# One comparison for both one-hots of an expert gate table, read by TensorE with a 32 byte step, and the table spread over eight weight tiles instead of twelve

## The chip, the cores and the metric

The kernel runs on one core of one Trainium2 chip. The metric is the device time of a whole run in microseconds (us). TensorE (PE, with its weight loads as PEld), VectorE (DVE), ScalarE (ACT), GpSimd (POOL) and the engine that issues weight transfers (SP) run side by side and wait for one another through semaphores.

## The reference, cut to what matters

The program is two transformer blocks on 512 tokens of width 1024. The change lies in the expert layer of the first block:

```python
scores = jnp.einsum('bshpc,hpnc->bshpn', q, sub_keys)        # 8 heads, 2 halves, 128 keys each
top_s, top_i = lax.top_k(scores, PEER_TOPK)                  # 16 best keys of each half
cand_i = top_i[..., 0, :, None] * 128 + top_i[..., 1, None, :]
best_s, best_pos = lax.top_k(cand_s, PEER_TOPK)              # 16 best pairs of each head
gate = jax.nn.softmax(best_s, axis=-1)
u = jnp.take(expert_u, ib, axis=0)                           # 128 experts for a token, of 16384
act = gelu(jnp.einsum('td,tkd->tk', xb, u))
y = jnp.einsum('tk,tkd->td', gb * act, jnp.take(expert_v, ib, axis=0))
```

## The kernel before

The first 128 tokens gather their expert rows. The other 384 (`ND`) run through all 16384 experts: `act` is computed densely as weight tiles times the tokens, and multiplied by a table of gates that is zero where a token did not choose an expert. This table is made one token at a time. A token has 128 choices (the partitions), each with a first key, a second key and a gate. With `hot1` the one-hot of the first key and `hot2` that of the second, the 128x128 matmul of `hot2` (the stationary operand) and `hot1` times the gate (the moving operand) gives the token's gates for all 16384 experts.

The stage `experts_u` streams 64 tiles of the first half of the work. One tile (`early_tile`, `part_u`, L1163 to L1183) is 24 fp32r matmuls of 128x384. Weights come from SP into a ring of four slots; ACT rounds a slot to its high part (`split_slot`, L795), POOL or DVE subtracts for the low part, and both parts are multiplied. ACT takes each finished tile through Gelu (`early_gelu`, L1932), splits the slot four tiles on and stores the result. The stage `experts` then streams further tiles in steps of six slots: two more tiles of activations (`late_tile`) and four slots of expert rows (`share`, L1230), which need the gates back from DRAM.

Meanwhile DVE picks the keys (`route_block`, four blocks of 128 tokens). PE transposes each block's keys and gates (`indices`, L1194), and DVE keeps them (`keep`, L2578) as `idx1`, `idx2` and `gate_t`. Tiles 0 to 51 run beside that. Tiles 52 to 63 (`G_TURN` = 13 turns of 4) carry the table, eight batches of four tokens in each: after every chunk of three matmuls, PE does four tokens (`g_batch`, L1209). A token's fp32 matmul shows as two MATMUL records. Batches go in groups of eight tokens, 48 groups in all, in double buffers:

- DVE (`hot_group`): first keys against `key_of`, all bf16, stored keys by tokens (L2703, 1024 elements); second keys against the key numbers in f32, stored tokens by keys (L2706, 1024 elements); then first one-hot times gate for four of the eight tokens (L2709, 512 elements), reading bf16 with a step of eight elements.
- ACT (`scale_hot`, L1960): the same product for the other four tokens, one instruction of 128 elements each, with the same step. Then it copies two batches of four tokens from PSUM to the staging buffer (L1976), and every fourth group it stores 2048 KB of gates (L1980).
- DVE also makes one low part of a weight slot per tile (`low_early_slot`, L2718), since POOL is occupied with gathers there.

DVE makes the constant `key_of` (L2722) just ahead of its first group. After the last group ACT waits for all stored gates and all stored activations, fetches the first gates and activations back (L1986, L1990), and only then takes the first `late_tile` through Gelu (L1999). PE's third late tile waits for that. DVE multiplies activations by gates (L2767) and makes low parts (L2772); the first `share` waits for these. Order on each engine is the program's order; every wait is a semaphore written by hand.

Of the kernel before, what the change touches and what calls it, by code (L numbers as in the profile page):

```python
# [36 lines left out]
P = 128  # L37
D = 1024
DC = D // P
# [76 lines left out]
GROUP = 2 * BATCH  # L116
QUAD = 4 * STEP
GBUFS = 6
SCALED = 4
DOT_STEPS = NSEL // 8  # L120
LOG_SEQ = 9
PADS = 5
# [45 lines left out]
def build(nc, c_d, ada_d, stream, consts_d, vecs_d, tables_d, x_d, keys_d, u_rows, v_rows, chunks_d, act_d, gates_d, out_d):  # L168
    with ExitStack() as ctx:
# [37 lines left out]
        def view(at, *dims, dt=F32, rows=P, of=None):  # L207
            n = int(np.prod(dims))
            of = of if of is not None else arena_r if dt == F32R else arena
            assert at + n <= of.shape[1], (at, dims, of.shape)  # L210
            a = of[0:rows, at:at + n]
            if dt == U32:
                a = a.bitcast(dt)
            if len(dims) == 2:
                a = a.rearrange("p (a b) -> p a b", b=dims[1])
            if len(dims) == 3:
                a = a.rearrange("p (a b c) -> p a b c", b=dims[1], c=dims[2])
            if len(dims) == 4:
                a = a.rearrange("p (a b c d) -> p a b c d", b=dims[1], c=dims[2], d=dims[3])
            return a  # L220
# [51 lines left out]
        yg = view(1056, D)  # L272
        routed = [view(1056 + 384 * k, 3, NSEL) for k in range(2)]
        pos_abf = view(1824, 2, NSEL)
        idx2 = view(2112, ND)
        gate_t = view(2496, ND)
        idx1 = place("idx1", [P, ND], BF16, at=at_arena + 2880)
        eidx = view(3264, NSEL, dt=U32)
        gate_g = view(3392, NSEL)
        act_g = view(3520, NSEL)  # L280
# [12 lines left out]
        keys = view(23656, QH, NKEYS)  # L293

        g_stage = [view(4448 + 4096 * k, NKEYS, STEP) for k in range(2)]
        hot2 = view(12640, 2, GROUP, NKEYS)
        hot1g = view(14688, 2, GROUP, NKEYS)
        hot1 = [place(f"hot1_{k}", [P, NKEYS, GROUP], BF16, at=at_arena + 16736 + 512 * k) for k in range(2)]
        key_of = place("key_of", [P, NKEYS, GROUP], BF16, at=at_arena + 17760)
        g_rows = [view(19552 + D * k, D) for k in range(GBUFS)]  # L300

        early = view(4448, 2, 2, ND)
# [208 lines left out]
        routed_ready = sem("routed_ready")  # L511
        eidx_ready = sem("eidx_ready")
        hot1_made = sem("hot1_made")
        hot_scaled = sem("hot_scaled")
        rows_in = [sem(f"rows_in{k}") for k in range(GBUFS)]
        rows_used = sem("rows_used")
        dots_taken = sem("dots_taken")
# [371 lines left out]
        def _(pe):  # L889
# [307 lines left out]
            for b in range(1, TB):  # L1197
                span(pe, INDEX_TURNS[b - 1], INDEX_TURNS[b], early_turn)
                indices(b)
            pe.wait_ge(h_row_ready, 1)  # L1200

            def g_batch(n, group, k):

                pe.wait_ge(hot_ready, group + (k // 2 + 1))
                pe.wait_ge(hot_scaled, group + (k // 2 + 1))
                wait(pe, g_kept, n + (k - 3))
                for t in range(BATCH):
                    at_t = BATCH * (k % 2) + t
                    last = pe.matmul(ps[:, k % 4, t * P:(t + 1) * P], hot2[:, k // 2 % 2, at_t, :],  # L1209
                                     hot1g[:, k // 2 % 2, at_t, :], start=True, stop=True)  # L1210
                last.then_inc(g_made, 1)

            def g_steps(i):
                for s in range(RING):
                    early_tile(i + G_TURN, s, lambda k: g_batch(i * 32 + DC * s, i * 16 + 4 * s, k))
            turns(pe, 3, g_steps)

            def late_tile(i, j, turn, s):
                wait(pe, gelu_done, i * 2 + (TILES + j - 1))
# [485 lines left out]
        def _(act):  # L1705
# [245 lines left out]
                act.activation(best[b % 2], best[b % 2], ACT.Exp).then_inc(gate_exp, 1)  # L1951


            def scale_hot(g):

                act.wait_ge(hot1_made, g + 1)
                wait(act, g_made, 2 * (g - 1))
                for t in range(SCALED):
                    k = GROUP * g + t
                    last = act.activation(hot1g[:, g % 2, t, :], hot1[g % 2][:, :, t], ACT.Identity,  # L1960
                                          scale=gate_t[:, k:k + 1])
                last.then_inc(hot_scaled, 1)

            groups = ND // GROUP
            scale_hot(0)
            for g in range(groups):
                step, n = g // 4, 2 * g
                if g % 4 == 0:
                    wait(act, g_saved[step % 2], 16 * (step // 2))
                if g + 1 < groups:  # L1970
                    scale_hot(g + 1)
                for k in (n, n + 1):
                    if k % DC == DC - 1:
                        early_gelu(G_TURN + step // RING, step % RING)
                    act.wait_ge(g_made, k + 1)
                    act.activation(g_stage[step % 2][:, :, BATCH * (k % DC):BATCH * (k % DC + 1)],  # L1976
                                   ps[:, k % 4, :].rearrange("p (t i) -> p i t", i=NKEYS), ACT.Copy).then_inc(g_kept, 1)
                if g % 4 == 3:
                    act.wait_ge(g_kept, n + 2)
                    act.dma_start(gates_d[:, step, :], g_stage[step % 2].rearrange("p i t -> p (i t)"))\  # L1980
                        .then_inc(g_saved[step % 2], 16)


            def fetch_gates(q):
# [20 lines left out]

            for k in range(2):
                act.wait_ge(g_saved[k], 16 * (STEPS // 2))
                act.wait_ge(act_saved[k], 16 * (TILES // 2))
            fetch_gates(0)
            fetch_acts(0)  # L2010
            for j in range(2):
                late_gelu(0, j, used(t0, j))
            for j in range(2):
                high_gated(j, late_hi[:, 0, j, :], late[:, j, :])
            for i in range(last_step):
                k0 = 2 + 6 * i
                p = i % 2
                wait(act, act_split, i * 4)
                fetch_acts(i + 1)
                if i == DOT_STEPS:  # L2020
                    act.wait_ge(rows_used, NSEL)
                    act.activation(act_g, act_g, ACT.Gelu).then_inc(dots_taken, 1)
                if p == 0 and i // 2 + 1 < TILES // 4:
                    fetch_gates(i // 2 + 1)
                split_expert(k0 + 2)
                split_expert(k0 + 3)
                for j in range(2):
                    high_gated(i * 4 + (2 + j), early_hi[:, j, :], early[:, p, j, :])
                for j in range(2):
                    late_gelu(i + 1, j, used(t0, k0 + j))  # L2030
                    split_expert(k0 + 4 + j)
                for j in range(2):
                    high_gated(i * 4 + (4 + j), late_hi[:, 1 - p, j, :], late[:, j, :])
                split_expert(k0 + 6)
                split_expert(k0 + 7)
# [316 lines left out]
        def _(dve):  # L2352
# [221 lines left out]
            def keep(b):  # L2574

                dve.wait_ge(routed_t, b)
                for k, dst in enumerate((idx1, idx2, gate_t)):
                    dve.tensor_copy(dst[:, (b - 1) * P:b * P], ps[:, 6, k * P:(k + 1) * P]).then_inc(routed_kept, 1)  # L2578

            steps = [0]  # L2580
# [23 lines left out]
            def route_block(b):  # L2604
# [79 lines left out]
                if b == 0:  # L2684
                    after()
                    dve.scalar_tensor_tensor(eidx, to[:, 0, :], float(NKEYS), to[:, 1, :], ALU.mult, ALU.add)\
                        .then_inc(eidx_ready, 1)

            for b in range(TB):
                route_block(b)  # L2690
                if b == TB - 1:
                    finish_gates(b)
                if b >= 2:
                    keep(b - 1)
            keep(TB - 1)

            def hot_group(g):

                t = slice(GROUP * g, GROUP * (g + 1))
                wide = [P, GROUP, NKEYS]  # L2700
                iota = cst("iota").unsqueeze(1).broadcast_to(wide)
                wait(dve, hot_scaled, g - 1)
                dve.tensor_tensor(hot1[g % 2][:, :, :], idx1[:, t].unsqueeze(1).broadcast_to([P, NKEYS, GROUP]), key_of[:, :, :],  # L2703
                                  ALU.is_equal).then_inc(hot1_made, 1)
                wait(dve, g_made, 2 * (g - 1))
                dve.tensor_tensor(hot2[:, g % 2], idx2[:, t].unsqueeze(2).broadcast_to(wide), iota, ALU.is_equal)  # L2706
                dve.wait_ge(hot1_made, g + 1)
                rest = slice(GROUP * g + SCALED, GROUP * (g + 1))
                dve.tensor_tensor(hot1g[:, g % 2, SCALED:, :], hot1[g % 2][:, :, SCALED:].rearrange("p j t -> p t j"),  # L2709
                                  gate_t[:, rest].unsqueeze(2).broadcast_to([P, GROUP - SCALED, NKEYS]), ALU.mult)\  # L2710
                    .then_inc(hot_ready, 1)

            def low_early_slot(k):

# [4 lines left out]
                    .then_inc(lo_ready, 1)  # L2719

            dve.wait_ge(routed_kept, 3 * (TB - 1))
            dve.tensor_copy(key_of[:, :, :], cst("iota").unsqueeze(2).broadcast_to([P, NKEYS, GROUP])).then_inc(routed_kept, 1)  # L2722
            dve.wait_ge(routed_kept, 3 * (TB - 1) + 1)
            for g in range(ND // GROUP):
                hot_group(g)
                if g % 4 == 1 and g > 4:
                    low_early_slot(g // 4 - 1)
            low_early_slot(ND // GROUP // 4 - 1)


            rows_done = [0]
# [585 lines left out]
```

## Time and profile before

| what | value |
|---|---|
| median of 3 runs | 3136.06 us (3135.14 to 3137.20) |
| span of the profiled execution, first to last instruction | 3134.2 us |
| PE busy / DVE / ACT / POOL | 95% / 65% / 40% / 37% |
| mean granted TensorE clock | 0.979 of full speed |

The page gives the span of the profiled execution and no separate time around it; the span is 1.9 us under the median of the runs. Busy shares are means over stages with quite different limits, so the stage that the change touches (from 738 us to 927 us of the span) is read by itself.

### The profile page before, as it was taken

The page shows a single profiled execution, that of the slowest core. Times are in us where ns is not written, and L with a number is a line of the kernel's source. Part 1 is how long each engine was busy: PE and PEld are TensorE (multiplying, and loading weights), DVE is VectorE, ACT ScalarE, POOL GpSimd, SP SyncE. Part 2 cuts the span into 40 slices and gives each one's busy share as a digit, 9 for nine tenths or more (in the row PEclk, how much of TensorE's full clock was granted, in tenths as well). Part 3 has the DMA queues.
Part 4 walks back from the last instruction along what each step waited for, and adds up shares of the span by engine and source line. Part 5 has one row for each costly group of instructions (what it writes and reads, how often), then busy time and mean ns, then how long its engine had stood idle before and what let it go on. Part 6 is the DMA issues. An engine that isn't in the chain of part 4 may idle for free.

```text
span 3134.2 us, 47541 instructions
## 1 busy us (share of the span) xinstructions
PE 2990.2 (95%) x17673; PEld 2612.4 (83%) x17673; DVE 2025.2 (65%) x3238; ACT 1261.6 (40%) x2075; POOL 1157.7 (37%) x564
## 2 busy tenths in 40 slices
PE   6999999998999999999999999899999998999998
PEld 3766679998988888888887788699999975799986
DVE  4767515999977778788886255466651375466622
ACT  3347333446963333333333334432222446432221
POOL 2420333664014444455553222044444430244442
PEclk9998999999999999999999999799999999999999
DMA  6710223555679999999996211023223420122231
GB/s 247 280 60 1 62 93 96 166 175 191 227 248 350 346 328 341 337 351 350 346 347 229 75 55 41 14 88 94 87 88 101 117 81 1 41 89 93 94 101 67
DMA packets 179876, 509.22 MB, mean 162 GB/s; under 512 B 14881, under 2 KB 72353, under 8 KB 175393
## 3 DMA queue, kind: packets, MB, share of 16 engines
q1 hardware_dynamic: 72288, 262.57, 25.4%
q0 software_dynamic: 37440, 136.40, 11.9%
q10 hardware_dynamic: 70016, 108.54, 10.3%
q8 instruction: 79, 1.29, 0.2%
q14 instruction: 53, 0.43, 0.0%
HBM read 467.60 MB, written 39.85 MB: 162 GB/s over the span
## 4 chain that ended last, share of the span: by engine, by line
PE 87%; ACT 5%; DVE 4%; issue 2%; DMA 1%; ACTq 0%; DVEq 0%
PE ps L1279 23%; PE ps L1230 17%; PE ps L1167 16%; PE ps L1533 8%; PE ps L901 8%; ACT arena L1960 2%; PE ps L1351 2%; PE ps L952 1%; ACT arena L1976 1%; PE ps L1680 1%; PE ps L1299 1%; PE ps L1457 1%; PE ps L1414 1%; PE ps L654 1%; PE ps L1421 1%
## 5 line engine op out<-in xcount | busy, mean ns | idle before, releaser
L2314 POOL TENSOR_TENSOR w_lo<-ring,w_hi 128x1024 fp32r<-128x1024 f32 x300 | 755.0, 2520 | 1387.9 <-ACT w_hi L795 1387.8
L795 ACT ACTIVATE w_hi<-ring 128x1024 fp32r<-128x1024 f32 x500 | 525.4, 1055 | 771.9 <-PE ps L1230 277.4
L1230 PE MATMUL ps<-w_hi,arena_r 128*128 128x512 f32 x1536 | 426.8, 397 | 4.5 <-DVE arena_r L2772 4.5
L1167 PE MATMUL ps<-h_hi,w_hi 128*128 128x384 f32 x1024 | 355.5, 347 | 5.0 <-issue 5.0
L1230 PEld LDWEIGHTS ps<-w_hi,arena_r 128*128 128x128 f32 x1536 | 289.0, 189 | 72.2 <-DVE arena_r L2772 5.0
L1167 PE MATMUL ps<-h_lo,w_hi 128*128 128x384 f32 x1024 | 348.9, 341 | 0.0
L1279 PE MATMUL ps<-h_hi,w_hi 128*128 128x264 f32 (+2 forms) x1536 | 347.5, 298 | 0.6 <-DVE arena L2869 0.5
L1167 PE MATMUL ps<-h_hi,w_lo 128*128 128x384 f32 x1024 | 346.4, 338 | 0.0
L1279 PE MATMUL ps<-h_lo,w_hi 128*128 128x264 f32 (+2 forms) x1536 | 346.2, 297 | 0.0
L1279 PE MATMUL ps<-h_hi,w_lo 128*128 128x264 f32 (+2 forms) x1536 | 345.6, 297 | 0.0
L2327 POOL DMA_INDIRECT arena<-u_rows,arena x128 | 193.4, 1511 | 375.8 <-DVE arena L2748 354.5
L2761 DVE TENSOR_TENSOR w_lo<-ring,w_hi 128x1024 fp32r<-128x1024 f32 x188 | 228.4, 1221 | 134.9 <-ACT w_hi L795 133.6
L2327 POOL DMA_INDIRECT arena<-v_rows,arena x128 | 206.6, 1614 | 174.8 <-DVE arena L2754 143.9
L1279 PEld LDWEIGHTS ps<-h_hi,w_hi 128*128 128x128 f32 x1536 | 246.6, 188 | 10.5 <-DVE arena L2869 0.9
L1279 PEld LDWEIGHTS ps<-h_hi,w_lo 128*128 128x128 f32 x1536 | 243.9, 189 | 7.5
L1279 PEld LDWEIGHTS ps<-h_lo,w_hi 128*128 128x128 f32 x1536 | 244.0, 188 | 6.6
L1230 PE MATMUL ps<-w_lo,arena_r 128*128 128x512 f32 x768 | 241.9, 397 | 0.0
L1533 PE MATMUL ps<-arena_r,w_hi 128*128 128x264 f32 (+1 forms) x1056 | 224.5, 321 | 0.0
L1167 PEld LDWEIGHTS ps<-h_hi,w_hi 128*128 128x128 f32 x1024 | 193.7, 189 | 6.6 <-issue 5.3
L1167 PEld LDWEIGHTS ps<-h_lo,w_hi 128*128 128x128 f32 x1024 | 193.9, 189 | 1.4
L1167 PEld LDWEIGHTS ps<-h_hi,w_lo 128*128 128x128 f32 x1024 | 194.3, 190 | 0.0
L1533 PEld LDWEIGHTS ps<-arena_r,w_hi 128*128 128x128 f32 x1056 | 163.3, 188 | 15.9
(343 smaller groups left out, 5444.0 us busy)
## 6 DMA issues: line engine op xcount, KB each, us to landing
ring<-weight_stream SPq DMA_DIRECT2D x500, 512.0 KB, 3.7
gates<-arena ACTq DMA_DIRECT2D x12, 2048.0 KB, 7.3
arena<-gates ACTq DMA_DIRECT2D x32, 768.0 KB, 14.3
arena<-w_modulation ACTq DMA_DIRECT2D x17, 1024.0 KB, 5.3
early_acts<-arena ACTq DMA_DIRECT2D x64, 192.0 KB, 2.7
arena<-early_acts ACTq DMA_DIRECT2D x32, 384.0 KB, 7.7
arena<-w_modulation ACTq DMA_DIRECT2D x2, 2560.0 KB, 15.0
x<-x_t ACTq DMA_DIRECT2D x1, 2112.0 KB, 19.5
```

Of the source, the lines that this page charges most:

```text
L654: last = pe.matmul(dst if n.T == SEQ else dst[:, b, :], lhsT, src[:, lo:hi], start=j == 0, stop=j == len(group) - 1)
L795: act.activation(w_hi[:, s, :], ring[:, s, :], ACT.Copy).then_inc(hi_ready, 1)
L901: last = pe.matmul(ps[:, bank, :], w, v, start=c == 0 and p == 0, stop=c == DC - 1 and p == 2)
L1167: last = pe.matmul(ps[:, bank, 0:ND], w, v, start=c == 0 and p == 0, stop=c == DC - 1 and p == 2)
L1230: last = pe.matmul(ps[:, Y_BANKS[b][half], :], a[u], w[v][:, half * BANK:(half + 1) * BANK], start=first and p == 0, stop=final and p == 2)
L1279: last = pe.matmul(ps[:, 2 * pair + b, 0:hi - lo], w, v[:, lo:hi], start=c == 0 and p == 0, stop=c == DC - 1 and p == 2)
L1351: last = pe.matmul(ps[:, v_bank(half, b), :], v, w, start=c == 0 and p == 0, stop=c == DC - 1 and p == 2)
L1533: last = pe.matmul(ps[:, 2 * (t % 2) + b, 0:hi - lo], w, v[:, lo:hi], start=c == 0 and p == 0, stop=c == FC - 1 and p == 2)
L1960: last = act.activation(hot1g[:, g % 2, t, :], hot1[g % 2][:, :, t], ACT.Identity, scale=gate_t[:, k:k + 1])
L2314: pool.tensor_tensor(w_lo[:, s, :], ring[:, s, :], w_hi[:, s, :], ALU.subtract)\
L2327: pool.indirect_dma_start(out=g_rows[n % GBUFS], out_offset=None, in_=table, in_offset=bass.IndirectOffsetOnAxis(ap=eidx[:, s:s + 1], axis ...
L2761: dve.tensor_tensor(w_lo[:, s, :], ring[:, s, :], w_hi[:, s, :], ALU.subtract).then_inc(lo_ready, 1)
```

## The change

- `idx1` and `idx2` are both kept as bf16 in one tile `idx12`. One comparison makes both one-hots of eight tokens (`compare_keys`, 2048 elements, bf16 in and out, keys by tokens).
- DVE multiplies all eight first one-hots by their gates (`scale_keys`, 1024 elements, read and written keys by tokens), and waits for the comparison of that group. ACT no longer scales; it widens the second one-hots to f32 with one copy of 1024 elements (`widen_hot`).
- `hot1g` and `hot2` are stored keys by tokens, so PE reads one token of either with a step of eight f32 elements (32 bytes), both as stationary and as moving operand.
- The table starts at tile 54 and takes eight tiles with twelve batches each. Tiles 52, 53, 62 and 63 carry none. ACT takes tiles 52 and 53 through Gelu before its first widening.
- `key_of` is made before `route_block(0)`. DVE's eight low parts go to every sixth group and four follow after the loop.
- After the table ACT fetches the first gates without waiting for all stored activations; for the first activations it waits for two stores, and for the others after the first late Gelu.

```diff
-        idx2 = view(2112, ND)
-        idx1 = place("idx1", [P, ND], BF16, at=at_arena + 2880)
+        idx12 = place("idx12", [P, 2, ND], BF16, at=at_arena + 2880)
+        key_of = place("key_of", [P, NKEYS, GROUP], BF16, at=at_arena + 3776)
-        hot2 = view(12640, 2, GROUP, NKEYS)
-        hot1g = view(14688, 2, GROUP, NKEYS)
+        hot2 = view(12640, 2, NKEYS, GROUP)
+        hot1g = view(14688, 2, NKEYS, GROUP)
+        hot = [place(f"hot{k}", [P, 2, NKEYS, GROUP], BF16, at=at_arena + 16736 + 1024 * k) for k in range(2)]
...
+            for s in range(2):
+                early_tile(G_TURN, s)
...
-                    last = pe.matmul(ps[:, k % 4, t * P:(t + 1) * P], hot2[:, k // 2 % 2, at_t, :],
-                                     hot1g[:, k // 2 % 2, at_t, :], start=True, stop=True)
+                    last = pe.matmul(ps[:, k % 4, t * P:(t + 1) * P], hot2[:, k // 2 % 2, :, at_t],
+                                     hot1g[:, k // 2 % 2, :, at_t], start=True, stop=True)
...
+                def batches(c):
+                    per = G_BATCHES // G_TILES
+                    for k in range(per * c // DC, per * (c + 1) // DC):
+                        g_batch(per * j + k)
...
-            def scale_hot(g):
-                act.wait_ge(hot1_made, g + 1)
-                wait(act, g_made, 2 * (g - 1))
-                for t in range(SCALED):
-                    k = GROUP * g + t
-                    last = act.activation(hot1g[:, g % 2, t, :], hot1[g % 2][:, :, t], ACT.Identity,
-                                          scale=gate_t[:, k:k + 1])
+            def widen_hot(g):
+                act.wait_ge(hot1_made, g + 2)
+                wait(act, g_made, 2 * (g - 1))
+                act.activation(hot2[:, g % 2], hot[g % 2][:, 1], ACT.Copy).then_inc(hot_widened, 1)
...
-            scale_hot(0)
+            for t in range(G_TURN * RING, G_FIRST):
+                early_gelu(t // RING, t % RING)
+            widen_hot(0)
...
-                act.wait_ge(act_saved[k], 16 * (TILES // 2))
             fetch_gates(0)
+            for k in range(2):
+                act.wait_ge(act_saved[k], 16)
             fetch_acts(0)
...
+            def compare_keys(g):
+                t = slice(GROUP * g, GROUP * (g + 1))
+                both = [P, 2, NKEYS, GROUP]
+                wait(dve, hot_widened, g - 1)
+                dve.tensor_tensor(hot[g % 2][:, :, :, :], idx12[:, :, t].unsqueeze(2).broadcast_to(both),
+                                  key_of[:, :, :].unsqueeze(1).broadcast_to(both), ALU.is_equal).then_inc(hot1_made, 1)
+            def scale_keys(g):
+                t = slice(GROUP * g, GROUP * (g + 1))
+                dve.wait_ge(hot1_made, g + 2)
+                wait(dve, g_made, 2 * (g - 1))
+                dve.tensor_tensor(hot1g[:, g % 2], hot[g % 2][:, 0],
+                                  gate_t[:, t].unsqueeze(1).broadcast_to([P, NKEYS, GROUP]), ALU.mult).then_inc(hot_ready, 1)
...
+            compare_keys(0)
+            lows = 3 * RING
             for g in range(ND // GROUP):
-                hot_group(g)
-                if g % 4 == 1 and g > 4:
-                    low_early_slot(g // 4 - 1)
+                scale_keys(g)
+                if g + 1 < ND // GROUP:
+                    compare_keys(g + 1)
+                if g % 6 == 2:
+                    low_early_slot(g // 6)
```

## Rows read from the trace of the kernel before

**Rows 1.** The page, busy time of each engine.

```profile
PE 2990.2 (95%) x17673; PEld 2612.4 (83%) x17673; DVE 2025.2 (65%) x3238; ACT 1261.6 (40%) x2075; POOL 1157.7 (37%) x564
```

**Rows 2.** Windows of the table: PE, PEld, DVE, ACT, POOL busy, clock, DMA share, GB/s.

```profile
752.00:754.00 2.00, 2.00 (x10) 2.00 (x9) 1.67 (x3) 1.24 (x3) 0.00 (x0) 0.50 0.00 0
826.00:839.00 13.00, 12.12 (x94) 11.80 (x93) 12.82 (x15) 12.51 (x29) 0.00 (x0) 1.00 0.59 219
```

**Rows 3.** The chain that ended last, 735 to 930 us: start, length, what.

```profile
831.02 0.96 ACT arena L1976 x2
831.99 1.67 ACT arena L1960 x4
...
902.04 8.46 PE ps L1167 x48
910.50 5.01 issue
915.50 11.34 PE ps L1167 x48
```

**Rows 4.** The same chain over the whole span, in the expert stage.

```profile
943.64 8.44 PE ps L1167 x48
```

**Rows 5.** Groups of instructions by form, 517 to 960 us.

```profile
L1209 PE MATMUL ps<-arena 128*128 128x128 f32 x768 | 103.6, 278 | 16.3 <-ACT arena L1960 7.1 <-DVE arena L2709 5.4 <-issue 3.8
...
L1960 ACT ACTIVATE arena<-hot,arena 128x128 f32<-128x128 bf16 x192 | 85.2, 522 | 13.3 <-DVE hot L2703 8.0 <-ACT arena L1976 5.3
...
L2706 DVE TENSOR_TENSOR arena<-arena,const 128x1024 f32<-128x1024 f32 x48 | 58.7, 1224 | 3.8 <-PE ps L1209 2.1
...
L2709 DVE TENSOR_TENSOR arena<-hot,arena 128x512 f32<-128x512 bf16 x48 | 51.7, 1078 | 0.0
L2703 DVE TENSOR_TENSOR hot<-idx,key_of 128x1024 bf16<-128x1024 bf16 x48 | 33.0, 687 | 0.0
...
L1951 ACT ACTIVATE arena<-arena 128x128 f32<-128x128 f32 x4 | 1.2, 310 | 0.0
```

**Rows 6.** Timeline of DVE in one table tile: start, length, engine, line.

```profile
829.18 1.21 DVE L2718 TENSOR_TENSOR w_lo<-ring,w_hi 128x1024 fp32r<-128x1024 f32 x1
830.31 0.68 DVE L2703 TENSOR_TENSOR hot<-idx,key_of 128x1024 bf16<-128x1024 bf16 x1
830.92 1.21 DVE L2706 TENSOR_TENSOR arena<-arena,const 128x1024 f32<-128x1024 f32 x1
```

**Rows 7.** Timeline of PE in one table tile.

```profile
831.26 1.15 PE L1209 MATMUL ps<-arena 128*128 128x128 f32 x8 [0.88 <-ACT arena L1960]
...
834.20 1.05 PE L1209 MATMUL ps<-arena 128*128 128x128 f32 x8
...
835.62 1.05 PE L1209 MATMUL ps<-arena 128*128 128x128 f32 x8
```

**Rows 8.** Timeline of ACT in one table tile.

```profile
827.22 1.06 ACT L795 ACTIVATE w_hi<-ring 128x1024 fp32r<-128x1024 f32 x1
...
828.16 0.60 ACT L1976 ACTIVATE arena<-ps 128x512 f32<-128x512 f32 x1
```

**Rows 9.** Timeline at the start of the table.

```profile
743.19 0.87 PE L1194 MATMUL ps<-const,arena 128*128 128x128 f32 x3 [5.02 <-DVE arena L2578]
...
744.82 2.69 DVE L2722 CAST key_of<-const 128x1024 bf16<-128x1024 f32 x1
...
750.39 2.08 PE L1209 MATMUL ps<-arena 128*128 128x128 f32 x8 [5.37 <-DVE arena L2709]
```

**Rows 10.** Timeline of ACT after the table.

```profile
903.14 0.33 ACTq L1980 DMA_DIRECT2D gates<-arena  x1
910.79 1.53 ACTq L1986 DMA_DIRECT2D arena<-gates  x2
```

**Rows 11.** Timeline of DVE after the table.

```profile
918.90 1.03 DVE L2767 TENSOR_TENSOR arena<-arena 128x384 f32<-128x384 f32 x2 [15.02 <-DMA arena<-gates]
...
925.32 1.02 DVE L2772 TENSOR_TENSOR arena_r<-arena,arena_r 128x384 fp32r<-128x384 f32 x2
```

More of the change, by code:

```diff
@@ L118 @@
 GBUFS = 6
-SCALED = 4
+G_TILES = 8
+G_FIRST = 54
 DOT_STEPS = NSEL // 8
@@ L295, in build @@
         g_stage = [view(4448 + 4096 * k, NKEYS, STEP) for k in range(2)]
-        hot2 = view(12640, 2, GROUP, NKEYS)
-        hot1g = view(14688, 2, GROUP, NKEYS)
-        hot1 = [place(f"hot1_{k}", [P, NKEYS, GROUP], BF16, at=at_arena + 16736 + 512 * k) for k in range(2)]
-        key_of = place("key_of", [P, NKEYS, GROUP], BF16, at=at_arena + 17760)
+        hot2 = view(12640, 2, NKEYS, GROUP)
+        hot1g = view(14688, 2, NKEYS, GROUP)
+        hot = [place(f"hot{k}", [P, 2, NKEYS, GROUP], BF16, at=at_arena + 16736 + 1024 * k) for k in range(2)]
         g_rows = [view(19552 + D * k, D) for k in range(GBUFS)]
@@ L513, in build @@
         hot1_made = sem("hot1_made")
-        hot_scaled = sem("hot_scaled")
+        hot_widened = sem("hot_widened")
         rows_in = [sem(f"rows_in{k}") for k in range(GBUFS)]
@@ L1199, in _, with g_batch, g_between @@
                 indices(b)
+            for s in range(2):
+                early_tile(G_TURN, s)
             pe.wait_ge(h_row_ready, 1)
[L1202 to L1206, printed above, removed]
+            def g_batch(k):
+                pe.wait_ge(hot_ready, k // 2 + 1)
+                pe.wait_ge(hot_widened, k // 2 + 1)
+                wait(pe, g_kept, k - 3)
                 for t in range(BATCH):
                     at_t = BATCH * (k % 2) + t
-                    last = pe.matmul(ps[:, k % 4, t * P:(t + 1) * P], hot2[:, k // 2 % 2, at_t, :],
-                                     hot1g[:, k // 2 % 2, at_t, :], start=True, stop=True)
+                    last = pe.matmul(ps[:, k % 4, t * P:(t + 1) * P], hot2[:, k // 2 % 2, :, at_t],
+                                     hot1g[:, k // 2 % 2, :, at_t], start=True, stop=True)
                 last.then_inc(g_made, 1)
[L1213 to L1216, printed above, removed]
+            def g_between(j):
+                def batches(c):
+                    per = G_BATCHES // G_TILES
+                    for k in range(per * c // DC, per * (c + 1) // DC):
+                        g_batch(per * j + k)
+                return batches
+            for j in range(G_TILES):
+                early_tile((G_FIRST + j) // RING, (G_FIRST + j) % RING, g_between(j))
+            for t in range(G_FIRST + G_TILES, TILES):
+                early_tile(t // RING, t % RING)
             def late_tile(i, j, turn, s):
@@ L1951, in _ @@
                 act.activation(best[b % 2], best[b % 2], ACT.Exp).then_inc(gate_exp, 1)
-            def scale_hot(g):
-                act.wait_ge(hot1_made, g + 1)
+            def widen_hot(g):
+                act.wait_ge(hot1_made, g + 2)
                 wait(act, g_made, 2 * (g - 1))
-                for t in range(SCALED):
-                    k = GROUP * g + t
-                    last = act.activation(hot1g[:, g % 2, t, :], hot1[g % 2][:, :, t], ACT.Identity,
-                                          scale=gate_t[:, k:k + 1])
-                last.then_inc(hot_scaled, 1)
+                act.activation(hot2[:, g % 2], hot[g % 2][:, 1], ACT.Copy).then_inc(hot_widened, 1)
             groups = ND // GROUP
-            scale_hot(0)
+            for t in range(G_TURN * RING, G_FIRST):
+                early_gelu(t // RING, t % RING)
+            widen_hot(0)
             for g in range(groups):
@@ L1970, in _ @@
                 if g + 1 < groups:
-                    scale_hot(g + 1)
+                    widen_hot(g + 1)
                 for k in (n, n + 1):
-                    if k % DC == DC - 1:
-                        early_gelu(G_TURN + step // RING, step % RING)
+                    per = G_BATCHES // G_TILES
+                    if k % per == per - 2:
+                        early_gelu((G_FIRST + k // per) // RING, (G_FIRST + k // per) % RING)
                     act.wait_ge(g_made, k + 1)
@@ L1981, in _ @@
                         .then_inc(g_saved[step % 2], 16)
+            for t in range(G_FIRST + G_TILES, TILES):
+                early_gelu(t // RING, t % RING)
             def fetch_gates(q):
@@ L2014, in _ @@
                 high_gated(j, late_hi[:, 0, j, :], late[:, j, :])
+            for k in range(2):
+                act.wait_ge(act_saved[k], 16 * (TILES // 2))
             for i in range(last_step):
@@ L2576, in keep @@
                 dve.wait_ge(routed_t, b)
-                for k, dst in enumerate((idx1, idx2, gate_t)):
+                for k, dst in enumerate((idx12[:, 0], idx12[:, 1], gate_t)):
                     dve.tensor_copy(dst[:, (b - 1) * P:b * P], ps[:, 6, k * P:(k + 1) * P]).then_inc(routed_kept, 1)
@@ L2687, in route_block @@
                         .then_inc(eidx_ready, 1)
+            dve.tensor_copy(key_of[:, :, :], cst("iota").unsqueeze(2).broadcast_to([P, NKEYS, GROUP])).then_inc(hot1_made, 1)
             for b in range(TB):
@@ L2695, in _ @@
             keep(TB - 1)
-            def hot_group(g):
+            def compare_keys(g):
                 t = slice(GROUP * g, GROUP * (g + 1))
[L2700 to L2704, printed above, removed]
-                wait(dve, g_made, 2 * (g - 1))
[L2706 to L2711, printed above, removed]
+                both = [P, 2, NKEYS, GROUP]
[5 more added lines that the diff above has]
+                dve.wait_ge(hot1_made, g + 2)
+                wait(dve, g_made, 2 * (g - 1))
+                dve.tensor_tensor(hot1g[:, g % 2], hot[g % 2][:, 0],
+                                  gate_t[:, t].unsqueeze(1).broadcast_to([P, NKEYS, GROUP]), ALU.mult).then_inc(hot_ready, 1)
             def low_early_slot(k):
@@ L2721, in _ @@
             dve.wait_ge(routed_kept, 3 * (TB - 1))
-            dve.tensor_copy(key_of[:, :, :], cst("iota").unsqueeze(2).broadcast_to([P, NKEYS, GROUP])).then_inc(routed_kept, 1)
-            dve.wait_ge(routed_kept, 3 * (TB - 1) + 1)
+            dve.wait_ge(hot1_made, 1)
+            compare_keys(0)
+            lows = 3 * RING
             for g in range(ND // GROUP):
-                hot_group(g)
-                if g % 4 == 1 and g > 4:
-                    low_early_slot(g // 4 - 1)
-            low_early_slot(ND // GROUP // 4 - 1)
+                scale_keys(g)
[3 more added lines that the diff above has]
+                    low_early_slot(g // 6)
+            for k in range(ND // GROUP // 6, lows):
+                low_early_slot(k)
             rows_done = [0]
```

## The prediction

> **What bounds the kernel now.** I read the page first. It says PE, 95% busy [rows 1], but that is a mean over all stages, so I read the stage of the change by itself, first in windows and in the chain, then on each engine's timeline.
>
> In a table tile PE, DVE and ACT are all nearly full: 12.12, 12.82 and 12.51 of 13 us [rows 2]. Which of them ends last is in the chain: ACT, with 1.67 us for four scalings and 0.96 us for two copies in every group [rows 3]. PE's own pace is a batch start to start when nothing is late: 835.62 - 834.20 = 1.42 us [rows 7]. Once or more in a tile PE waits, as 0.88 us on ACT's scaling [rows 7]. From the first table matmul at 750.39 [rows 9] to the last at 902.04 [rows 3] are 151.7 us; 96 batches of 1.42 us are 136.3. So 15.4 us are lost inside the table.
>
> Two more losses lie around it. At the start PE waits 5.02 us for routing (that stays), does the transposes at 743.19, and then waits 5.37 us more for the first group, while DVE makes `key_of` in 2.69 us [rows 9]; its clock is still 0.50 at 752 to 754 us, the lower of its two levels (1.2 and 2.4 GHz), and 1.00 later [rows 2]. At the end the last gates leave at 903.14 and the fetch goes out at 910.79 [rows 10], with ACT's Gelu queued behind it, so PE idles 5.01 us; its next two tiles take 11.34 us where two such tiles in the expert stage take 8.44 [rows 3, 4]. These 2.9 us are the price of the slow clock after a pause. In the expert stage the chain is PE work alone [rows 4], so what is saved here should come through to the end whole.
>
> **Part by part.** *PE.* A chunk of three weight matmuls is 3 x 8.46/48 = 0.529 us [rows 3]. A token costs (1.42 - 0.529)/4 = 0.223 us, and each of its two records 0.111 us. The count of both stays, so PE's work from tile 52 to 63 stays 136.3 us, if reading with a 32 byte step costs nothing. Not one PE operand before has such a step, so I bound it. DVE reads bf16 with a 16 byte step in L2709. Its fixed part comes from L2706 and L2703: 1224 - 687 = 537 ns is half of 1024 elements' streaming in f32, so 1.05 ns each and 150 ns fixed. L2709 then takes (1078 - 150)/512 = 1.81 ns for an element [rows 5]. ACT takes 522 ns for 128 such elements, against 310 for 128 adjacent ones: 1.66 ns more on top of about 0.9, so 2.55 [rows 5, 8]. PE streams adjacent fp32r at 0.176/384 = 0.46 ns [rows 3] and this fp32 table at 0.111/128 = 0.87 ns. The two ends: by ratio, DVE's slowing of 1.7 on PE's best rate is 0.79 ns, below 0.87, so nothing is added (there is no reason for a gain); by absolute time, ACT's 2.55 ns makes a record 0.326 us, and 768 records [rows 5] cost 768 x 0.215 = 165 us. I take nothing, because the table's fp32 stream asks for elements only about half as often as PE is seen to read them; but this is the weak step.
>
> "Need at least two hits on a cacheline to absorb SRAM access latency", says the Trainium skill (Advanced Engine Details and Errata, SBUF Cachelines), with lines of 16 bytes. By that rule a 32 byte step pays; the DVE and ACT rows agree for their 16 byte step, and no row here shows it for TensorE. It gives no size; with DVE's row for the price, the sum would be about 3204 us instead of 3113.5.
>
> *DVE.* Away go a bf16 comparison (0.61 us start to start), an f32 comparison (1.13, as any plain 1024 here) [rows 6] and the stepped product (1078 ns) [rows 5]. In come a comparison of 2048 bf16 elements, 150 + 2 x 537 = 1224 ns, if it keeps the double rate of L2703, and a product of 1024 adjacent elements at 1.13. The product now waits for the comparison just ahead of it, so that one counts in full, with an allowance of 0.04 us to wake. A group is 1.13 + 1.26 = 2.39 us; six are 14.3, and the low part adds 1.13 but hides one wait: 15.3 us a tile. PE's new tile is 8 x 0.529 + 48 x 0.223 = 14.9. DVE is late by 0.4 a tile, 3.2 in eight; double buffers let it be 2.49 - 1.22 = 1.3 us ahead at most. I take 2 us.
>
> *ACT.* A group is one copy of 1024 (0.94 us, the pitch of L795 [rows 8]) and two of 512 (0.96 [rows 3]): six are 11.4, with Gelu (0.35 by its 384 elements), split (0.94) and the gate store 13.6 of 14.9 us. After the Gelu of a tile the widening of the group after next comes 5.0 us after PE ends the tile, and PE wants it after about 4.6; that is within the allowance for DVE. Nothing.
>
> *Start.* `key_of` moves to where DVE waits for the first scores, which costs nothing; without that pause it would be 2.69 us in front of the routing. Tiles 52 and 53 fill PE's 5.37 us. PE starts them cold: 2.9 us lost, as after the other pause. But ACT's first widening is now queued behind tile 53's Gelu and split, 0.35 + 0.94 + 1.06 = 2.4 us after that tile, and PE has one chunk of 0.53 to cover it: 1.9 us lost.
>
> So from the end of the transposes at 743.7 (743.19 and about 0.5): 136.3 + 2.9 + 1.9 + 2 = 143.1 us, where 902.04 - 743.7 = 158.3 were spent. Saved: 15.2.
>
> *End.* The store of the last gates takes 903.14 to 910.79, 7.65 us, and now lies beside tiles 62 and 63 (8.46 us). ACT then has tile 63's Gelu and split, fetches at about 10 us after tile 61, and the first late Gelu comes at about 14, while PE wants it after four tiles, 16.9. The fetch to the second early low part took 926.34 - 910.79 = 15.6 us [rows 10, 11]; so the first `share` is ready at 25.5 and PE has six tiles, 25.4. DVE's 15.02 us of waiting for gates [rows 11] becomes harmless. From the last table matmul to the first share PE needed 8.46 + 5.01 + 11.34 = 24.8; now 16.9 and 0.5 for collisions with the store. Saved: 7.4. Stores of gates (12) and activations stay the same in number, in 119 us instead of 152; SP and POOL get their low parts two tiles ahead as before.
>
> Sum: 3136.1 - 15.2 - 7.4 = 3113.5 us, on the median; the span it is read from is 1.9 us less.
>
> **Rivals.**
> 1. *TensorE pays for the step* (ends slower). For it: two engines of two that read a 16 byte step pay. Against it: PE's fp32 stream is at half its seen rate. If a record doubles, 768 x 0.111 = +85 and DVE's 2 us vanish: 3197. By DVE's 1.81 ns a record is 0.232: +93, 3204. By ACT's ratio of 2.8 on 0.46 ns it is 0.165: +42, 3153. By ACT's absolute time 3277. It decides from 22.6/768 = 29 ns a record, 1.1 ns an element. The cacheline rule of the Trainium skill (page and section above) speaks for this rival.
> 2. *The merged comparison loses the double rate.* Then 150 + 2048 x 1.05 = 2300 ns; a group 3.47, 48 of them and eight low parts 174.6 against PE's 119.2: +55 for the 2: 3167. Against it: the same operand pattern runs at it in L2703 [rows 5], with one dimension less.
> 3. *The saving is smaller.* The engines, again within 10% of one another, go on waiting in turn and lose the 15.4 us again: 3127. Or the fetch still ends last: 7.4 back, 3121.
>
> **How the numbers follow.** The forecast 0.53, its own range 3104 to 3122 (DVE never late, no end collision, and less cold time below; ACT late by 0.5 a tile and 2 us at the end above). Rival 1 0.36, rival 2 0.04, rival 3 0.05, others 0.02. The range must take in doubling and DVE's price: 3104 to 3205 leaves out under 0.04 below and 0.11 above. A measurement here tells about 0.2%, 6 us. Faster: 0.53 and most of rival 3, 0.57. Slower: rivals 1 and 2 without their mildest cases, 0.39. Same: 0.04.
>
> **What the profile of the changed kernel would show.** The matmul records of the table line start 0.11 us apart, or 0.2 and more: this alone decides the sign. The merged comparison takes 1.22 us and not 2.3; the product 1.22; ACT's widening 1.06. PE has no idle time from the transposes to tile 54's first chunk, then some 1.9 us for ACT. Between table and first share it shows no pause and no fall of the clock. The forecast is wrong if PE's records stretch, or if the widening rather than DVE's product ends last in each group.

## The result, and the profile after

The changed kernel takes 3215.11 us (median of 4 runs, 3211.62 to 3219.31) where the kernel before takes 3135.6 us: 1.0256 times as long, 95% interval 1.0243 to 1.0269. It is slower by 2.6%, outside the range that was forecast. The forecast had the sign wrong.

The groups of instructions after, 517 to 1040 us (count, then busy us, mean ns, idle before); they stand against those of the products and comparisons before [rows 5]:

```profile
L1211 PE MATMUL ps<-arena 128*128 128x128 f32 x768 | 196.7, 422 | 2.0 <-ACT arena L1968 2.0
...
L1211 PEld LDWEIGHTS ps<-arena 128*128 128x128 f32 x768 | 189.0, 336 | 2.3 <-issue 2.3
...
L2717 DVE TENSOR_TENSOR hot<-idx,key_of 128x2048 bf16<-128x2048 bf16 x48 | 60.6, 1262 | 4.7 <-ACT arena L1968 4.7
L2725 DVE TENSOR_TENSOR arena<-hot,arena 128x1024 f32<-128x1024 bf16 x48 | 58.8, 1226 | 95.1 <-PE ps L1211 95.0
L1985 ACT ACTIVATE arena<-ps 128x512 f32<-128x512 f32 x96 | 57.3, 597 | 103.2 <-PE ps L1211 103.2
L1968 ACT ACTIVATE arena<-hot 128x1024 f32<-128x1024 bf16 x48 | 50.4, 1052 | 5.3 <-ACT arena L1985 5.3
```

The new work of DVE and ACT costs what was forecast: comparison 1262 ns (1224 forecast), product 1226 ns (about 1220), widening 1052 ns (1060). The double rate of the bf16 comparison is there. But TensorE's table records have grown from 278 to 422 ns each, its weight loads for the table from 193 to 336, and DVE and ACT now wait for PE in place of the reverse: 95.0 and 103.2 us of idle time.

The chain that ended last after, start and length, through the stage:

```profile
742.03 9.93 PE ps L1167 x48
753.32 1.05 ACT arena L1968
754.51 2.25 PE ps L1211 x8
756.76 0.96 PE ps L1167 x3
757.73 3.78 PE ps L1211 x16
...
853.90 3.87 PE ps L1211 x16
...
974.68 8.43 PE ps L1167 x48
...
984.74 10.19 DMA arena<-gates
...
1002.48 7.74 PE ps L1240 x32
```

Sixteen records in 3.87 us are 0.242 us each, against 0.111 before. 768 x 0.131 = 100.6 us. In the chain before, ACT held most of the table [rows 3]; now PE holds it all. A window of the table says the same, with the clock at 1.00 (PE, PEld, DVE, ACT, POOL busy, clock, DMA share, GB/s), and two of the first microseconds of the table show the clock partly or wholly at its lower level:

```profile
754.00:757.00 3.00, 2.49 (x10) 2.52 (x11) 1.23 (x1) 1.51 (x3) 0.00 (x0) 0.74 0.02 5
757.73:758.70 0.97, 0.97 (x5) 0.97 (x5) 0.00 (x0) 0.00 (x0) 0.00 (x0) 0.50 0.00 0
850.00:866.00 16.00, 16.00 (x72) 15.98 (x71) 8.32 (x8) 8.46 (x13) 0.00 (x0) 1.00 0.26 110
```

PE and its loads are full for all 16 us; DVE and ACT are at 8.32 and 8.46.

The early rows say one thing more. For the first 0.97 us of the 16 records that start at 757.73 the clock stood at 0.50, and DVE and ACT did nothing; yet the 16 took 3.78 us, no more than the 3.87 at full clock. The chunk of three weight matmuls just before took 0.96 us where 0.53 is the pace at full clock. So the stepped record does not stretch with the granted clock, as it would if its 0.242 us were so many cycles of TensorE (by estimate that would have added about 0.5 us).

The measure used from here on is the time from the transposes of the last block (L1194) to the first matmul of the first `share`: 743.19 to 926.7 before, 183.5 us; 741.16 to 1002.5 after, 261.3 us. The difference, 77.8 us, is nearly the whole of the difference of the medians, 79.5, so what happens in the stage does pass to the end whole. It stands in this table for every run, beside the start-to-start time of one record in the gate table. A ratio is to runs of the kernel before taken beside it, whose median was 3135.2 to 3137.3 us; the four kernels with one run have none.

| kernel | median us | ratio to before, 95% interval | stage us | record us |
|---|---|---|---|---|
| before | 3135.6 | | 183.5 | 0.111 |
| after, both operands at 32 bytes | 3215.1 | 1.0256 (1.0243 to 1.0269) | 261.3 | 0.242 |
| e2, stationary alone at 32 bytes | 3208.2 (1 run) | | 254.9 | 0.234 |
| e3, moving alone at 32 bytes | 3209.1 (1 run) | | 254.2 | 0.233 |
| e5, both at 16 bytes | 3211.7 (1 run) | | 257.6 | 0.238 |
| e4, both at 8 bytes | 3118.9 (1 run) | | 168.2 | 0.1175 |
| e8, the same again | 3122.2 | 0.9951 (0.9937 to 0.9964) | 169.6 | 0.1175 |
| e1, adjacent for PE, stepped for the writers | 3154.0 | 1.0059 (1.0046 to 1.0073) | 200.7 | 0.111 |
| e6, 8 bytes, twelve tiles | 3128.9 | 0.9973 (0.9962 to 0.9984) | 174.5 | 0.1175 |
| e7, 8 bytes, widening earlier | 3120.8 | 0.9949 (0.9936 to 0.9963) | 165.9 | 0.1175 |
| e9, 8 bytes, tiles 53 to 60 | 3119.8 | 0.9942 (0.9928 to 0.9955) | 165.6 | 0.1175 |

Single runs of one kernel lie up to 9 us from their median, much of it through time outside the stage (the profiled runs of e4 and e8, the same kernel, took 3118.85 and 3131.3 us with 168.2 and 169.6 in the stage), so differences of a few microseconds are read in the stage column.

### The profile page after: what moved, and what is told of

Same layout as the page of the kernel before. It is cut to its first block, busy times and chain, and to the rows that moved or that the text cites. A ratio compares the mean times of both kernels' runs of the same rounds, so it can differ in the third digit from the quotient of the medians.

```text
span 3210.7 us, 47292 instructions
## 1 busy us (share of the span) xinstructions
PE 3085.4 (96%) x17673; PEld 2711.3 (84%) x17673; DVE 2004.4 (62%) x3190; ACT 1235.3 (38%) x1931; POOL 1153.7 (36%) x564
## 4 chain that ended last, share of the span: by engine, by line
PE 91%; DVE 4%; ACT 2%; DMA 1%; issue 1%; ACTq 0%; DVEq 0%
PE ps L1289 23%; PE ps L1240 17%; PE ps L1167 16%; PE ps L1543 8%; PE ps L901 8%; PE ps L1211 6%; PE ps L1361 2%; PE ps L952 1%; PE ps L1690 1%; PE ps L654 1%; PE ps L1309 1%; PE ps L1467 1%; PE ps L1424 1%; PE ps L1431 1%; PE ps L1450 1%
## 5 line engine op out<-in xcount | busy, mean ns | idle before, releaser
L2341 POOL DMA_INDIRECT arena<-v_rows,arena x128 | 205.6, 1606 | 174.5 <-DVE arena L2773 143.6
L1211 PE MATMUL ps<-arena 128*128 128x128 f32 x768 | 196.7, 422 | 2.0 <-ACT arena L1968 2.0
```

The lines of the kernel that those rows point to most:

```text
L2341: pool.indirect_dma_start(out=g_rows[n % GBUFS], out_offset=None, in_=table, in_offset=bass.IndirectOffsetOnAxis(ap=eidx[:, s:s + 1], axis ...
```

## The experiments

All keep the arithmetic of the changed kernel. What is varied in each is first the layout of the two f32 tables: `hot2` and `hot1g` become runs of S tokens. TensorE then reads a token with a step of 4 x S bytes: S = 8 is the changed kernel, S = 1 gives adjacent keys.

```diff
-        hot2 = view(12640, 2, NKEYS, GROUP)
+        hot2 = view(12640, 2, GROUP // S, NKEYS, S)
-  hot2[:, k // 2 % 2, :, at_t]
+  hot2[:, k // 2 % 2, at_t // S, :, at_t % S]
-  act.activation(hot2[:, g % 2], hot[g % 2][:, 1], ACT.Copy)
+  act.activation(hot2[:, g % 2].rearrange("p a j s -> p j a s"),
+                 hot[g % 2][:, 1].rearrange("p j (a s) -> p j a s", s=S), ACT.Copy)
```

and the same for `hot1g` with DVE's product. What PE computes is the same in all of them; only the places of the elements differ.

### e1: adjacent keys for TensorE (S = 1 for both)

> The changed kernel, but ACT's widening and DVE's product write their tables tokens by keys, so that PE reads adjacent elements and the step of 512 bytes is on the writing side. Theory A (TensorE pays for reading with a 32 byte step: its table records start 0.242 us apart after the change against 0.111 before, and 768 x 0.131 = 101 us is the whole miss): records back at 0.111 us, 3215 - 101 = 3114 us, which is the prediction without its weak step. Rival B (the records are long for another reason, such as keys by tokens being in the same SBUF lines that DVE and ACT write at that time): they stay above 0.2 us, near 3215. Rival C (the writers pay for a stepped write as they do for a stepped read, 1.81 ns an element on DVE): DVE's group is 1.26 + 2.0 = 3.3 us, 48 groups 157 + 8 low parts against PE's 119, so about 3155.

Measured: 3154.0 us, and the groups of instructions of this run, 740 to 1000 us:

```profile
L1211 PE MATMUL ps<-arena 128*128 128x128 f32 x768 | 103.7, 282 | 29.0 <-issue 14.5 <-DVE arena L2726 11.4 <-ACT arena L1968 2.9
L1968 ACT ACTIVATE arena<-hot 128x1024 f32<-128x1024 bf16 x48 | 99.4, 2074 | 7.0 <-PE ps L1211 5.3 <-DVE hot L2718 0.9
L2726 DVE TENSOR_TENSOR arena<-hot,arena 128x1024 f32<-128x1024 bf16 x48 | 98.0, 2042 | 4.9 <-PE ps L1211 3.6
```

PE's timeline has the pace of a batch with no wait in it:

```profile
845.72 1.05 PE L1211 MATMUL ps<-arena 128*128 128x128 f32 x8
...
847.14 2.11 PE L1211 MATMUL ps<-arena 128*128 128x128 f32 x16
```

A batch is again 847.14 - 845.72 = 1.42 us start to start, and a record 0.111 us, as before [rows 7]; its mean length is 282 ns (278 before). So the records on TensorE are as theory A has them, and B falls: the read step is what made them long. (Shared lines could not have done it: the writers fill one half of the double buffer while PE reads the other.) But the time is not 3114. The step has moved to the writers, and they pay as rival C said: DVE's product takes 2042 ns in place of 1226, (2042 - 150)/1024 = 1.85 ns an element, and ACT's widening 2074 in place of 1052. In the chain DVE's product and comparison now follow each other, 3.06 us a group. PE waits for DVE's product (11.4 us). The step has a price on whichever side it stands. That the time fell on rival C's 3155 within 1 us is partly chance: its own terms (157 + 9 - 119 us on 3114, less the 2 us that the 3114 already held for DVE's lateness) give about 3159, and a group took 3.06 us and not 3.3.

### e2 and e3: one operand alone (S = 8 and S = 1)

> Only the stationary operand (second keys) is read with the 32 byte step, the moving one is adjacent. Theory A1 (each of the two streams is limited by itself at 1.89 ns an element and loads lie beside the matmuls): records 0.242 us apart, 3215. Rival A2 (the moving stream alone pays): 0.111, 3114. Rival A3 (both pay and the costs add up): half, about 0.177, 3165.

> Only the moving operand (first keys times gates) is read with the 32 byte step. A1: 0.242 us a record, 3215. A2: also 0.242, 3215. A3: 0.177, 3165. If it is 0.111 here, the loads alone pay.

Measured: 3208.2 and 3209.1 us. One row of the chain of e2, then of e3:

```profile
799.70 3.75 PE ps L1211 x16
```

```profile
801.22 3.73 PE ps L1211 x16
```

That is 0.234 and 0.233 us a record: each stepped stream by itself is nearly as slow as both together (0.242). Theory A1 holds; that the moving stream alone pays (A2) and that the costs add up (A3) are both out. Loads lie beside matmuls, and the slower of the two sets the pace, so leaving one of the operands adjacent helps almost nothing. The groups of the two runs, 740 to 1000 us, e2 first, show which is which: the loads are long (334 ns) where the stationary operand is the stepped one and nearly as in e1 (207 against 195) where it is not.

```profile
L1211 PEld LDWEIGHTS ps<-arena 128*128 128x128 f32 x768 | 188.1, 334 | 2.3 <-issue 2.3
L2726 DVE TENSOR_TENSOR arena<-hot,arena 128x1024 f32<-128x1024 bf16 x48 | 95.8, 1995 | 57.2 <-PE ps L1211 56.4
```

```profile
L1211 PEld LDWEIGHTS ps<-arena 128*128 128x128 f32 x768 | 157.2, 207 | 18.7 <-issue 3.2
L1968 ACT ACTIVATE arena<-hot 128x1024 f32<-128x1024 bf16 x48 | 97.2, 2028 | 5.3 <-ACT arena L1986 5.3
```

They also repeat e1's reading: DVE's product, the only one that writes with the long step in e2, takes 1995 ns; ACT's widening in e3 2028.

### e4, e5 and e8: a step of 8 and of 16 bytes

> Both operands are read with a step of 8 bytes (pairs of tokens adjacent), two elements to every 16 bytes. Theory D (what costs is 16 bytes fetched per 1.89 ns, so two elements in 16 bytes take 0.94 ns each against the 0.87 ns that the fp32 stream wants): records 0.121 us, 3114 + 768 x 0.010 = 3122. Theory E (any step loses adjacency and costs the same): 0.242, 3215.

> Both operands are read with a step of 16 bytes (four tokens adjacent), one element to every 16 bytes. Theory D (one 16 byte piece of SBUF per 1.89 ns and stream): the same as the 32 byte step, records 0.242 us apart, 3215 us. Rival F (the cost grows with the length of the step, from 0.1175 at 8 bytes to 0.242 at 32): about 0.16 to 0.18, 3150 to 3165.

> The fourth run's kernel timed in rounds. 3119 us again (3116 to 3122), faster than the kernel before by 0.55%. If the single time was a chance low, it lies nearer to 3136 than 3125.

Measured: 3118.9 us for 8 bytes, 3211.7 for 16, and 3122.2 for 8 bytes again (median of 6 runs), 0.9951 of the kernel before. In e4 the keys of a token lie 8 bytes apart, two in every 16 bytes, with those of another token between them. The chain of e4, then of e5:

```profile
842.78 1.88 PE ps L1211 x16
...
880.85 9.22 DMA gates<-arena
...
890.80 9.04 DMA arena<-gates
...
907.51 17.07 PE ps L1240 x72
```

```profile
773.51 3.80 PE ps L1211 x16
```

It gives 1.88/16 = 0.1175 us a record at 8 bytes (theory D: 0.121), 3.80/16 = 0.238 at 16. Doubling the step from 8 to 16 bytes doubles the time of a record, and doubling it again to 32 adds nothing that matters. So rival F (the cost grows with the length) and theory E (any step costs the same) fall. What the runs fit is one 16 byte piece of SBUF per about 1.9 ns and stream: with two wanted elements in a piece an element takes 0.92 ns, close to the 0.87 ns of the fp32 stream of adjacent keys; with one in a piece 1.86 to 1.89. The size of 16 bytes is what fits, and is not measured by itself: the runs show that a step of 8 bytes is nearly free and one of 16 costs as much as one of 32. "Need at least two hits on a cacheline to absorb SRAM access latency" (the Trainium skill, Advanced Engine Details and Errata, SBUF Cachelines): these runs agree for TensorE, and give the price that the section does not. What inside the memory or the engines sets this pace the runs do not tell, but for the one thing that the pace does not follow TensorE's granted clock (3.78 us for 16 records, part of them at 0.50). The writers of e4, which store two adjacent elements and then hop 1 KB, pay little, DVE 5 ns of 1226 and ACT 126 ns of 1052:

```profile
L2726 DVE TENSOR_TENSOR arena<-hot,arena 128x1024 f32<-128x1024 bf16 x48 | 59.1, 1231 | 7.2 <-PE ps L1211 5.7
L1968 ACT ACTIVATE arena<-hot 128x1024 f32<-128x1024 bf16 x48 | 56.5, 1178 | 5.9 <-ACT arena L1986 3.4 <-PE ps L1211 1.9 <-DVE hot L2718 0.2
```

### e6: the table over twelve tiles again, at 8 bytes

```diff
-G_TILES = 8
-G_FIRST = 54
+G_TILES = 12
+G_FIRST = 52
```

and DVE's low parts again in every fourth group, and ACT's Gelu again where the kernel before has it, at a tile's last batch.

> Step of 8 bytes as in the fourth run, but the table again over twelve tiles from tile 52, eight batches in each, so that only the spread is undone. If the spread is worth what the prediction says, the pause at the end comes back (5.0 us idle and 2.9 of slow clock, against 2.4 us in front of the first share now: +5.5) and PE waits some 4.5 us with nothing to do for the first group, against 2.5 for ACT's widening now: 3119 + 7.5 = 3126 us. Rival (the spread is worth nothing and all the gain is the lighter work of DVE and ACT): 3119.

Measured: 3128.9 us, stage 174.5. Against e4 and e8 (168.2 and 169.6) the spread is worth 5 to 6 us of the stage, a little less than the 7.5 expected; that it is worth nothing (3119) is out. All the rest of the change together, which is the lighter DVE and ACT work, `key_of` made earlier and the fetches with fewer waits, is worth 183.5 - 174.5 = 9.0 us, with the step's 768 x 0.0065 = 5 us already paid. No run parts these three. Two rows of PE's timeline show the two pauses that eight tiles cover, where e4 waits 2.1 us at the start and 2.0 at the end:

```profile
749.29 2.05 PE L1209 MATMUL ps<-arena 128*128 128x128 f32 x8 [4.45 <-ACT arena L1966]
...
905.96 0.66 PE L1167 MATMUL ps<-h_hi,w_hi 128*128 128x384 f32 x1 [5.23 <-issue]
```

### e7 and e9: ACT's first widening earlier, and the table one tile earlier

```diff
-            for t in range(G_TURN * RING, G_FIRST):
-                early_gelu(t // RING, t % RING)
-            widen_hot(0)
+            early_gelu(G_TURN, 0)
+            widen_hot(0)
+            early_gelu(G_TURN, 1)
```

> Step of 8 bytes, and ACT widens the first group between the Gelus of tiles 52 and 53, not behind both. The wait of PE for ACT ahead of the first table matmul (2.1 us, after which the clock is at the lower level again for some microseconds) goes away: 3119 - 2.1 - about 2 = 3115 us. Rival: the second group's widening, still behind tile 53's Gelu and split, takes its place within one batch: 3118.

Measured: 3120.8 us, not 3115; ratio and median as e8's within the scatter. In the stage PE no longer waits for ACT at the start of the table, as expected, and the stage takes 165.9 us against 168.2 and 169.6: 2.3 to 3.7 us less, where 4 were expected. (PE waits 1.4 to 1.6 us once more behind the table in e7 and in e8, but not in e4, so the 3.7 against e8 compares like with like.)

> Step of 8 bytes, the table on tiles 53 to 60 and ACT's first widening ahead of tile 52's Gelu, so that three plain tiles lie behind the table. In the seventh run the chain into the first share was the store of the last gates (9.6 us) and their fetch (10.3), and PE waited for it about 3 us. If one more tile of 4.2 us covers that, PE takes 163 us from the transposes to the first share instead of 165.9, about 3118 us in all. Rival: at the start the widening is not ready after one tile, and what is won at the end is lost there: 166 us, 3121.

Measured: 3119.8 us, stage 165.6. The start was not lost (0.47 us of waiting for ACT) but nothing was won at the end either. The chain of e9 after the table:

```profile
873.26 12.65 PE ps L1167 x72
...
886.32 0.47 ACT w_hi L795
...
886.89 0.61 ACTq L1996
...
887.54 9.95 DMA arena<-gates
```

The store of the gates is no longer in the chain; tile 63's Gelu and split on ACT now stand ahead of the fetch in ACT's order, so a plain tile more behind the table covers nothing; PE still waits 2.58 us ahead of the first share. The expectation had not counted with this. Of all kernels here e9 has the lowest ratio, 0.9942 (0.9928 to 0.9955), not to be told from e7 and e8.

## Why the prediction was wrong, by its own steps

- **PE, "reading with a 32 byte step costs nothing".** This is the step that failed, and the only large one. The bound from both sides held it: 0 and 165 us, with DVE's absolute 1.81 ns an element for +93; measured +100.6, 1.89 ns an element, and e1, with adjacent keys, has the 0.111 us record back. The choice between the ends was wrong. The prediction scaled DVE's slowing by PE's best rate, as if a step halved the rate of whichever engine reads. The runs show a time per 16 byte piece that is about the same for DVE's read (1.81), DVE's write (1.85) and PE's two reads (1.82 to 1.89); only ACT's read was slower (2.55) [rows 5]. The rows of before already had DVE's value. That the fp32 stream asks for elements only half as often as TensorE can read them gave no slack. Rival 1 was given 0.36 and had, by DVE's price, 3204 us. Its variant by doubling is wrong as a mechanism, though near in size (0.222 against 0.242).
- **DVE.** Comparison and product came as costed (1262 and 1226 ns). The 2 us for DVE's lateness were not there: in the changed kernel PE is slower than DVE, and in e4, where its own work is near that forecast, PE waits in the table 3.0 us in all, none of it for DVE by the trace. Rival 2 is out.
- **ACT.** Widening 1052 ns against 1060; past its first one it never holds the table.
- **Start.** Tiles 52 and 53 fill the pause. They took 9.93 us where 8.46 is the pace at full clock, so the slow clock cost 1.5 us and not the 2.9 forecast. The wait for ACT's first widening was forecast as 1.9 us and came as 2.03; that the clock would fall again after it, 0.74 of full speed in 754 to 757 us, was not forecast and cost about 0.7 us (the first chunk 0.96 us for 0.53, the first batch 2.25 for 1.95).
- **End.** No long pause, but the first share starts at 1002.48 where 974.68 + 25.35 = 1000.03 would be free of waits: 2.45 us lost, not 0.5. The fetch went out at 9.4 us after the table, about as forecast, but from its issue to DVE's first instruction on the gates passed 10.9 us (984.09 to 994.95), against 8.1 before [rows 10, 11]. Those 2.8 us are about what is lost. In e6, where PE again pauses while the gates come back, the transfer took 8.29 us, against 10.19 here; why it is slower here was not tested.
- **Sum.** The small terms were 7.3 us forecast and 1.5 + 2.0 + 0.7 + 2.45 = 6.7 measured. Without the step's price the stage would be 261.3 - 100.6 = 160.7 us, where the forecast is 183.5 - 22.6 = 160.9. That the two agree to 0.2 us is partly luck: the small terms missed by 0.7 to 2 us each, two downwards (the slow clock by 1.4, DVE by 2) and two upwards (the end by 2, the clock's second fall by 0.7), and nearly cancelled.

No kernel here has a median of 3113.5. As long as the comparison is stored keys by tokens and TensorE takes one token at a time, the step has to stand somewhere. Pairs of tokens (e4) make it nearly free on both sides, for 5 us. A layout without the step on either side was not tried.

## What to carry to other kernels

Where a layout moves a step from one engine to another, price it by the 16 byte pieces touched and not by the engine's usual pace: here about 1.8 to 1.9 ns for each piece with a single wanted element, reading or writing on DVE and reading on each of TensorE's two streams, and 2.55 ns for ACT's read. Two f32 to a piece were enough to make it nearly free: adjacent ones for the writers, and one left out between them for TensorE. When the only price at hand is another engine's absolute time, take it as it stands before scaling it.

## What the runs showed of the hardware beyond that

- A stepped stationary operand alone slows the stream of small fp32 matmuls as much as a stepped moving one: 0.234 and 0.233 us a record, 0.242 with both.
- The first merged comparison took 3.25 us where the other ones take 1.26. GpSimd was at a low part when it began. Here the wait was covered. DVE's and GpSimd's timelines after:

```profile
737.92 7.04 POOL L2328 TENSOR_TENSOR w_lo<-ring,w_hi 128x1024 fp32r<-128x1024 f32 x3
742.79 3.25 DVE L2717 TENSOR_TENSOR hot<-idx,key_of 128x2048 bf16<-128x2048 bf16 x1
...
747.22 1.22 DVE L2717 TENSOR_TENSOR hot<-idx,key_of 128x2048 bf16<-128x2048 bf16 x1
```

  The comparison ends at 746.04, 1.08 us after GpSimd does (744.96). In the traces of e1 to e9 it is 1.08 or 1.09 us as well, though GpSimd ends anywhere from 743.1 to 750.3 us there and the comparison takes 3.22 to 3.25. It looks as if the comparison did most of its work only when GpSimd was through; no run was made with GpSimd idle at that place. `key_of` fits: 2.69 us beside GpSimd before [rows 9], 0.68 after, at 415.4 us, where GpSimd does nothing.
- A wait of PE of 2.0 us, with the clock at 1.00 before it, was followed by a stretch with the clock at 0.74 on the mean (754 to 757 us), and in e4 by one at 0.80 (752 to 755); the wait of 0.88 us in the table before [rows 7] was not (clock 1.00) [rows 2]. The length of the wait alone does not decide it. Ahead of the first share the changed kernel waits 2.48 us and the clock stays at 1.00 (1002.5 to 1009 us), while e8 waits 2.05 us there and falls to 0.50 (918 to 920 us).
